# Heads of an mLSTM: weights divided by their denominators before the value products, shared source blocks added and multiplied once

## The chip, the cores and the metric

One core of a Trainium2 chip runs the whole program. The metric is the device time of one execution in microseconds (us). TensorE (PE) multiplies, VectorE (DVE), ScalarE (ACT) and GpSimd (POOL) work element by element, SyncE (SP) and the other queues start DMAs. PEld is the loading of weights into TensorE, which overlaps its matmuls.

## What is computed

The reference is a two-layer network over 256 context and 1024 latent tokens. The part that matters is the second layer's mLSTM: 4 heads of width 512, each scanned forwards and backwards, both directions after the context. In chunks the reference does, per head and direction,

```
s   = (q k^T) * exp(dmat - m_t)            # weights of target t over sources s
num = s @ v  (+ the carried state)
den = sum(s)  (+ the carried state)
h   = num / max(|den|, exp(-m_t))
hm  = h_forward + flip(h_backward)         # prefix_bidir
hn  = (hm - mean(hm)) * rsqrt(var(hm) + eps)   # head_norm, over the head's 512 columns
```

and then `(hn * g + skip * x) * silu(z)` is multiplied by `w_out`.

## The kernel before

The kernel does not carry a state: for each head it forms all weights of a target over all its sources (full quadratic form, with decays). Targets are the 1024 latent tokens in 4 groups q of 256 (`QW`), each of two blocks j of 128. Sources are 10 blocks of 128 tokens, in 5 pairs p: pair 0 is the context, pairs 1 to 4 the latent tokens. A context block is a source in both directions; a latent block before the target's is a source forwards only, one after it backwards only; the target's own block is a source in both, masked. So `sources(q, j, d)` has 13 entries over both directions d, for 10 different blocks.

Every product in fp32 is made of three products of rounded halves (`PARTS`: high*high, high*low, low*high). ACT makes the high part (`high`, L1512) and DVE the low part, full minus high (`low`, L2220). So the weights exist three times in SBUF: `PR` (p_full), `PH` (p_part0), `PL` (p_part1), each with two halves z = q % 2 of 26 pieces of 128 columns.

The head loop (`head` in each engine's program, 4 heads, heads 1 and 2 in a hardware loop) is written out by hand in the same order on every engine:

- `score(i, q, p)`: PE, 24 matmuls of 256 columns: one pair of source blocks against 256 targets, into one of three rotating PSUM banks (`SLOTS`, `LOB`; a slot may be written when what lay three slots before has been read). `value(i, n)` and `queries(i, q)` make values and queries in the same slots, in among the scores of q = 0 and 1 (queries of the next head at the end of the head).
- `weigh(q, p)`: DVE multiplies the scores by the decays into `PR` (L2325 for the target's own pair, L2327 for the others). `sum_up(i, q)`: POOL adds the pieces to `Sp`, one row of sums for each direction (9 instructions for each q, L2619 and L2629).
- `weights_high` (ACT) and `weights_low` (DVE): parts of the weights, each pair one step behind its `weigh`.
- `value_sums(i, q, j)`: PE, 13 entries x 3 parts = 39 matmuls of 512 columns, the two directions into two PSUM banks. `weight_sums`: two fp32 matmuls by a column of ones, the denominators, one column each.
- `head_out(q, j)`: DVE makes the reciprocal of the denominators (L2336 to L2338), ACT scales the forward bank (L1605), DVE adds the scaled backward bank (L2340), `bn_stats` (L2343) and `bn_aggr`, ACT a square root (L1608), DVE normalises (L2354).
- `transposed(i, q, j)` (PE, L1132) and `mixed(i, q, j)` (DVE, L2407, L2410) bring the result out, in among the scores of a later q.
- POOL's `masked` (L2606) and ACT's `decays` (L1587, L1590) prepare the decays of a later q. DVE's `columns_low` and ACT's `columns_high_in` make the parts of the next head's inputs near the end of a head.

The order on PE in one head: scores of q = 0, of q = 1, both value sums of q = 0, then for q = 2 and 3 five scores and both value sums of q - 1, then the queries of the next head around the value sums of q = 3.

## Time and profile before

| what | value |
|---|---|
| time, median of 3 | 2986.97 us (2985.12 to 2987.44) |
| the profiled execution | 2982.24 us |
| its span, first to last instruction | 2980.2 us |
| TensorE busy | 92% of the span |
| VectorE, ScalarE, GpSimd busy | 52%, 28%, 34% |
| mean granted TensorE clock | 0.949 |

The heads lie between about 2118 and 2770 us. In each row of a timeline stand the start in us, the duration, the engine, the line, the operation, output and inputs by name, shape and count; what is in brackets is how long the engine sat idle before it, and what ended that. A run of like instructions stands as one row. An fp32 matmul (not of rounded parts) is recorded as two matmuls.

### The profile page before, as it was taken

Reading aid. Unit: us, or ns where it says so; the run is one execution under the profiler, and the core shown is the slowest. Engines: PE = TensorE matmul, PEld = TensorE weight load, DVE = VectorE, ACT = ScalarE, POOL = GpSimd, SP = SyncE. Lnnn points to the kernel's source line nnn. Section 1 sums busy time; section 2 is a strip of 40 time slices with the busy share of each in tenths; the row PEclk is TensorE's granted clock in tenths of the full one; section 3 lists DMA queues with packets and bytes.
Section 4 is the critical chain, followed back from the end, with each engine's and each line's share of the span. In section 5 each row is a group of like instructions: output and inputs, shape, how many; then the busy total and the mean of one; then the engine's idle time right before and its main releaser. Section 6 shows DMA issues by size and latency. Waiting matters only on the chain.

```text
span 2980.2 us, 38078 instructions
## 1 busy us (share of the span) xinstructions
PE 2748.7 (92%) x13429; PEld 2132.8 (72%) x13429; DVE 1544.2 (52%) x2331; ACT 843.0 (28%) x1004; POOL 1027.7 (34%) x1181
## 2 busy tenths in 40 slices
PE   7998778999898999989995999999899999999998
PEld 5656764444454777878883777777798888888787
DVE  2336875678777121452326444585546555555611
ACT  1213551625625111321213222211323333231310
POOL 0006996878820001021123333343434334333000
PEclk8799889999999998899997999999999999999999
DMA  4512221011013667452103222256313121313521
GB/s 151 178 64 84 85 80 60 21 46 46 28 46 101 198 187 239 117 179 73 32 25 87 99 99 99 92 169 227 138 40 109 65 98 56 114 43 128 167 84 47
DMA packets 258722, 297.92 MB, mean 100 GB/s; under 512 B 34944, under 2 KB 222632, under 8 KB 258224
## 3 DMA queue, kind: packets, MB, share of 16 engines
q1 hardware_dynamic: 203104, 206.75, 21.8%
q10 hardware_dynamic: 50672, 72.89, 6.7%
q0 software_dynamic: 4832, 16.78, 1.9%
q8 instruction: 69, 1.13, 0.2%
q14 instruction: 45, 0.37, 0.0%
HBM read 203.09 MB, written 93.29 MB: 99 GB/s over the span
## 4 chain that ended last, share of the span: by engine, by line
PE 62%; DVE 12%; issue 5%; ACT 3%; POOL 1%; DMA 1%; DVEq 0%; SPq 0%; ACTq 0%; POOLq 0%
PE ps L130 53%; PE ps L1178 5%; PE ps L1027 1%; PE ps L1021 1%; DVE s_scan_tmp L1926 1%; DVE s_scan_tmp L1924 1%; DVE arena L1928 1%; DVE arena L1946 1%; DVE arena L1977 1%; DVE xc_part L2220 1%; DVE arena L1970 1%; DVE arena L485 1%; POOL h_part L2558 0%; PE ps L1183 0%; ACT arena L1342 0%
## 5 line engine op out<-in xcount | busy, mean ns | idle before, releaser
L130 PE MATMUL ps<-arena,weights 128*128 128x512 f32 (+2 forms) x2432 | 753.7, 488 | 51.1 <-ACT arena L1342 19.5
L130 PEld LDWEIGHTS ps<-arena,weights 128*128 128x128 f32 (+1 forms) x2432 | 398.6, 177 | 394.8 <-issue 325.1
L130 PE MATMUL ps<-h_part,in_weight_parts 128*128 128x512 f32 (+1 forms) x1920 | 419.2, 379 | 38.7 <-DVE h_part L1719 14.9
L130 PEld LDWEIGHTS ps<-h_part,in_weight_parts 128*128 128x128 f32 x1920 | 342.0, 192 | 111.3 <-issue 24.3
L130 PE MATMUL ps<-v_part,p_part 128*128 128x512 f32 x1248 | 295.1, 395 | 0.1
L130 PEld LDWEIGHTS ps<-v_part,p_part 128*128 128x128 f32 x1248 | 234.2, 190 | 49.2 <-issue 0.9
L130 PE MATMUL ps<-q_part,xc_part 128*128 128x256 f32 x1920 | 248.1, 288 | 14.7 <-DVE v_part L2220 10.7
L130 PEld LDWEIGHTS ps<-q_part,xc_part 128*128 128x128 f32 x1920 | 237.7, 195 | 16.3 <-DVE v_part L2220 11.5
L1178 PE MATMUL ps<-wo_part,mx_part 128*128 128x512 f32 x768 | 184.0, 400 | 5.2 <-DVE mx_part L2220 4.6
L2547 POOL TENSOR_TENSOR in_weight_parts<-weights,ones 128x1024 fp32r<-128x1024 f32 x32 | 79.2, 2474 | 305.6 <-issue 212.8
L1178 PEld LDWEIGHTS ps<-wo_part,mx_part 128*128 128x128 f32 x768 | 145.4, 191 | 40.0 <-issue 4.8
L2629 POOL TENSOR_TENSOR decays<-decays,p_full 128x256 f32<-128x256 f32 (+1 forms) x128 | 150.6, 1176 | 63.6 <-DVE p_full L2327 36.3
L130 PE MATMUL ps<-ao_part,out_weight_parts 128*128 128x512 f32 (+1 forms) x576 | 116.7, 363 | 8.1 <-DVE ao_part L2004 8.1
L130 PE MATMUL ps<-bo_part,out_weight_parts 128*128 128x512 f32 (+1 forms) x576 | 116.3, 362 | 4.4 <-DVE bo_part L2004 4.4
L2460 POOL TENSOR_TENSOR arena<-arena 128x640 f32 x16 | 31.7, 1979 | 251.0 <-DVE arena L1841 246.1
L2052 DVE SCALAR_TENSOR_TENSOR arena<-ps,modulation,arena 128x256 f32 (+3 forms) x32 | 32.6, 1060 | 159.8 <-PE ps L130 159.8
L130 PEld LDWEIGHTS ps<-ao_part,out_weight_parts 128*128 128x128 f32 x576 | 97.1, 192 | 25.6 <-issue 8.3
L130 PE MATMUL ps<-y_part,out_weight_parts 128*128 128x512 f32 (+1 forms) x576 | 114.9, 362 | 0.0
L1999 DVE COPY arena<-arena 64x1280 f32 x16 | 26.0, 1626 | 168.7 <-PE ps L130 168.4
L130 PE MATMUL ps<-arena 128*128 128x160 f32 (+2 forms) x608 | 108.5, 323 | 4.9 <-ACT arena L1454 2.9
L130 PEld LDWEIGHTS ps<-bo_part,out_weight_parts 128*128 128x128 f32 x576 | 96.4, 190 | 22.2 <-DVE bo_part L2004 2.7
L130 PEld LDWEIGHTS ps<-y_part,out_weight_parts 128*128 128x128 f32 x576 | 96.8, 191 | 17.9
(354 smaller groups left out, 4194.8 us busy)
## 6 DMA issues: line engine op xcount, KB each, us to landing
weights<-in_e_w_in SPq DMA_DIRECT2D x32, 512.0 KB, 4.2
weights<-in_o_w_in SPq DMA_DIRECT2D x32, 512.0 KB, 4.1
s_out_maps<-arena ACTq DMA_DIRECT2D x16, 640.0 KB, 3.0
weights<-in_mod_w POOLq DMA_DIRECT2D x20, 512.0 KB, 4.8
arena<-s_out_maps SPq DMA_DIRECT2D x16, 640.0 KB, 4.3
ml_xcv<-arena ACTq DMA_DIRECT2D x16, 640.0 KB, 3.0
xc_full<-ml_xcv SPq DMA_DIRECT2D x4, 2560.0 KB, 8.9
xm_tiles<-ml_xm SPq DMA_DIRECT2D x16, 640.0 KB, 3.9
```

The lines of the kernel that those rows point to most:

```text
L130: return nc.tensor.matmul(o, lhsT, rhs, start=(k == 0), stop=(k == n - 1))
L485: link(V.scalar_tensor_tensor(out=o, in0=o, scalar=1.0 / (2 * c + 1), in1=z2, op0=ALU.add, op1=ALU.mult))
L1021: nc.tensor.matmul(psG[:, t0:t0 + n], WFs[:, s, 0], xco[:, s, t0:t0 + n], start=False, stop=False, skip_group_check=True)
L1027: last = nc.tensor.matmul(psG[:, t0 + o:t0 + o + r.shape[1]], WFs[:, s, 1], r, start=False, stop=False, skip_group_check=True)
L1178: nc.tensor.matmul(ps[:, 2 * (b % 4) + h], Mbs[x][b % 2][:, k], Wos[w][k][:, BANK * h:BANK * h + BANK], start=(k == 0 and n == 0), stop=Fa ...
L1924: V.tensor_tensor(s2[:, ::-1], z, A2h, ALU.mult).then_inc(sem("scan_v"), 1)
L1926: V.tensor_tensor(s1, s1, s2, ALU.add).then_inc(sem("scan_v"), 1)
L1928: V.tensor_tensor(w, w, s1, ALU.add).then_inc(sem("scan_v"), 1)
L2052: V.scalar_tensor_tensor(out=o, in0=a, scalar=MOD[:, bass.ds(4 * i + (2 * (16 + s) + w), 1)], in1=x, op0=ALU.mult, op1=ALU.add).then_inc(s ...
L2460: GP.tensor_tensor(Gv[s][:, :, 0], pw(0), cc(0), ALU.mult)
L2547: GP.tensor_tensor(WXs[s][:, 0], Wv[:, s], ones[:, :].unsqueeze(1).to_broadcast([P, DT, P]), ALU.mult).then_inc(sem("w_high"), 1)
L2629: GP.tensor_tensor(Sp[:, z, s0:s1], Sp[:, z, s0:s1], PR[:, z, o:o + s1 - s0], ALU.add).then_inc(sem("sums"), 1)
```

## The change

The weights are divided by their denominators before they are multiplied by the values. Then the two directions can be added: for a source block that both directions use, the two weight pieces are added and multiplied by the values once.

- PE: `value_sums` has 10 blocks x 3 parts = 30 matmuls, all into one bank (2 + 2 (q % 2) + j). `weight_sums` becomes `denominators(i, q)`, the same four matmuls by a column, into a slot bank "d", ahead of the value sums. New is `denominator_rows(i, q)`: an fp32 matmul of 512 columns, ones times a 128x512 tile with the reciprocals on diagonals, so that each reciprocal stands in a row over all partitions, in a slot bank "r".
- DVE: `reciprocals(q)` (three small instructions and the diagonals `DG`, 128x512), `rows_out(q)` (PSUM to `RR`, 128x512), `scale_shared(q)` (weights of the pairs 0 and q + 1 times the rows: 1024, 512 and 256 columns), `merge_shared(q)` (additions of 512, 128 and 128 columns, and the other three pairs times their row, 512 each). `weights_low` works on 512 columns for every pair (before 1024, 768 and 3 x 512). In `head_out` the reciprocals and the addition of the directions go; `bn_stats` and the normalisation read PSUM.
- ACT: `weights_high` 5 x 512 columns for each q, from the scaled weights; the scaling in `head_out` goes, the square root stays (`spread`).
- The parts of the weights of q are no longer made one step behind `weigh(q, p)`: those of q = 0 are made after the queries of q = 3, those of q = 1 and 2 in among `weigh(q + 1, p)`, those of q = 3 between the value sums of q = 2.
- 48 slots in a head instead of 40.

```diff
+            def denominator_rows(i, q):
+                pe.wait_ge(*past("den_diag", 4 * i + (q + 1)))
+                mm(slot(i, "r", q), ones[:, :], DG, 0, 1).then_inc(sem("lo_mm"), 1)
+
+            def value_sums(i, q, j, first=0, end=NBLK):
+                if j == 0 and first == 0:
                     pe.wait_ge(*past("pl_ready", 20 * i + (5 * q + 5)))
...
+                for I in range(first, end):
+                    c = QW * (I % 2) + P * j
+                    x = (PH[:, q % 2, QW * (I - I % 2) + c:QW * (I - I % 2) + c + P], PL[:, q % 2, PAIR_AT[q][I // 2][0] + c:PAIR_AT[q][I // 2][0] + c + P])
+                    for m, (a, b) in enumerate(PARTS):
+                        last = mm(ps[:, 2 + 2 * (q % 2) + j], x[a], Vs_[b][:, I], 3 * I + m, 3 * NBLK)
...
                 for p in range(NPR):
                     value(i, p + 6)
                     score(i, 1, p)
+                    if p == 0:
+                        denominators(i, 0)
+                    elif p == 1:
+                        denominator_rows(i, 0)
                 value(i, 11)
                 queries(i, 3)
-                weighted(i, 0)
                 for q in (2, 3):
+                    value_sums(i, q - 2, 0)
+                    denominators(i, q - 1)
+                    value_sums(i, q - 2, 1)
+                    denominator_rows(i, q - 1)
                     for p in range(NPR):
                         score(i, q, p)
                         if p in (2, 4):
                             transposed(i, q - 2, p // 2 - 1)
-                    weighted(i, q - 1)
+                value_sums(i, 2, 0, 0, NBLK // 2)
+                denominators(i, 3)
+                value_sums(i, 2, 0, NBLK // 2, NBLK)
+                denominator_rows(i, 3)
+                value_sums(i, 2, 1)
+                value_sums(i, 3, 0)
                 if not last_head:
                     queries(i + 1, 0)
-                value_sums(i, 3, 0)
                 transposed(i, 2, 0)
...
# ACT, head()
+                for n in range(6, 12):
+                    value_high(i, n)
                 queries_high(i, 3)
+                for n in range(NPR):
+                    weights_high(i, 0, n)
                 decays(i, 3)
...
# DVE
+                def scale_shared(q):
+                    z, a, b = q % 2, PAIR_AT[q][0][0], PAIR_AT[q][q + 1][0]
+                    dve.wait_ge(*past("vq_ev", NEV * i + EVICTED["r", q]))
+                    dve.wait_ge(*past("sums", 36 * i + (9 * q + 9)))
+                    x = PR[:, z, a:a + 4 * QW].rearrange("p (d i t) -> p d i t", d=2, i=2)
+                    V.tensor_tensor(x, x, rd.unsqueeze(2).to_broadcast([P, 2, 2, QW]), ALU.mult)
+                    V.tensor_tensor(PR[:, z, b:b + 2 * QW], PR[:, z, b:b + 2 * QW], RR, ALU.mult)
+                    ilink(V.tensor_tensor(PR[:, z, b + 2 * QW:b + 3 * QW], PR[:, z, b + 2 * QW:b + 3 * QW], RR[:, P:P + QW], ALU.mult))
...
                 for p in range(NPR):
+                    if p == 2:
+                        rows_out(0)
                     value_low(p + 6)
                     weigh(1, p)
+                    if p == 0:
+                        reciprocals(0)
+                    elif p == 2:
+                        scale_shared(0)
+                    elif p == 3:
+                        merge_shared(0)
                 value_low(11)
...
-                weights_low(1, NPR - 1)
-                for q in (0, 1):
-                    head_out(q, 0)
-                    head_out(q, 1)
+                for n in range(NPR):
+                    weights_low(0, n)
+                for q in (1, 2):
+                    head_out(q - 1, 0)
+                    reciprocals(q)
+                    head_out(q - 1, 1)
+                    rows_out(q)
                     for p in range(NPR):
-                        weigh(q + 2, p)
+                        weigh(q + 1, p)
+                        if p == 0:
+                            scale_shared(q)
+                        elif p == 1:
+                            merge_shared(q)
                         if p in (2, 4):
-                            mixed(i, q, p // 2 - 1)
-                    weights_low(q + 2, NPR - 1)
+                            mixed(i, q - 1, p // 2 - 1)
+                        if p in (2, 3):
+                            weights_low(q, 2 * p - 4)
+                            weights_low(q, 2 * p - 3)
+                    weights_low(q, 4)
+                reciprocals(3)
                 head_out(2, 0)
+                rows_out(3)
+                scale_shared(3)
+                merge_shared(3)
+                for n in range(NPR):
+                    weights_low(3, n)
+                head_out(2, 1)
                 if not last_head:
                     maps_low(i + 1)
                     columns_low(i + 1)
-                head_out(2, 1)
```

## Rows read from the trace of the kernel before

**Rows 1.** Busy time by stretch: length, engines with counts, clock, DMA share, GB/s.

```profile
2450.00:2610.00 160.00, 152.06 (x978) 138.16 (x978) 90.14 (x189) 50.84 (x86) 60.09 (x56) 0.99 0.24 81
```

**Rows 2.** Waits in the heads, PE: us in total, times, longest.

```profile
PE ps L130 <- DVE v_part L2220: 14.4, 7, 3.3
```

**Rows 3.** Groups: count | busy us, mean ns of one | idle before them.

```profile
L130 PE MATMUL ps<-v_part,p_part 128*128 128x512 f32 x1248 | 295.1, 395 | 0.1
```

**Rows 4.** Timeline, head 1, PE: value sums of q 0, scores of q 2.

```profile
2338.04 9.13 PE L130 MATMUL ps<-v_part,p_part 128*128 128x512 f32 x39
...
2347.01 0.50 PE L130 MATMUL ps<-ones,decays 128*128 128x1 f32 x4
...
2347.37 9.15 PE L130 MATMUL ps<-v_part,p_part 128*128 128x512 f32 x39
...
2356.72 8.88 PE L130 MATMUL ps<-q_part,xc_part 128*128 128x256 f32 x72
...
2371.97 9.12 PE L130 MATMUL ps<-v_part,p_part 128*128 128x512 f32 x39
```

**Rows 5.** Timeline, earlier stage: fp32 matmuls of 512 columns, each recorded twice.

```profile
1881.90 1.02 PE L1021 MATMUL ps<-arena 128*128 128x512 f32 x2
1882.76 1.02 PE L1027 MATMUL ps<-arena 128*128 128x512 f32 x2
```

**Rows 6.** Timeline, head 1, DVE: from the statistics of q 0 onwards.

```profile
2359.06 0.69 DVE L2343 BATCH_NORM_STATS2 att_small<-weights 128x6 f32<-128x512 f32 x1
...
2360.60 1.00 DVE L2354 TENSOR_SCALAR weights<-weights,s_scan_tmp 128x512 f32<-128x512 f32 x2
2361.52 2.43 DVE L2327 SCALAR_TENSOR_TENSOR p_full<-ps,att_small,decays 128x256 f32<-128x256 f32 x6
...
2367.33 0.69 DVE L2220 TENSOR_TENSOR p_part<-p_full,p_part 128x512 fp32r<-128x512 f32 x1 [0.66 <-POOL decays L2629]
2367.94 0.68 DVE L2407 TENSOR_TENSOR weights<-ps,weights 128x512 f32<-128x512 f32 x1
```

**Rows 7.** Groups of VectorE, by shape.

```profile
L2220 DVE TENSOR_TENSOR p_part<-p_full,p_part 128x512 fp32r<-128x512 f32 x48 | 34.9, 726 | 8.5 <-POOL decays L2629 5.5 <-ACT p_part L1512 2.9
...
L2220 DVE TENSOR_TENSOR p_part<-p_full,p_part 128x1024 fp32r<-128x1024 f32 x16 | 19.5, 1220 | 5.6 <-POOL decays L2619 5.6
...
L2354 DVE TENSOR_SCALAR weights<-weights,s_scan_tmp 128x512 f32<-128x512 f32 x32 | 16.0, 543 | 0.6
...
L1701 DVE COPY arena<-ps 128x512 f32<-128x512 f32 x16 | 10.5, 687 | 23.6 <-PE ps L770 23.6
```

**Rows 8.** Timeline, head 3, PE: queries of q 2 to the first value sum.

```profile
2632.11 1.66 PE L130 MATMUL ps<-xc_part,qk_map_part 128*128 128x256 f32 x12
...
2636.04 3.10 PE L130 MATMUL ps<-q_part,xc_part 128*128 128x256 f32 x24 [1.37 <-DVE q_part L2260]
...
2642.48 3.13 PE L130 MATMUL ps<-q_part,xc_part 128*128 128x256 f32 x24 [2.45 <-DVE v_part L2220]
...
2658.42 9.10 PE L130 MATMUL ps<-v_part,p_part 128*128 128x512 f32 x39
```

**Rows 9.** Timeline, head 1, PE: value sums of q 2 to the next head.

```profile
2405.89 9.12 PE L130 MATMUL ps<-v_part,p_part 128*128 128x512 f32 x39
...
2440.20 0.60 PE L130 MATMUL ps<-ones,decays 128*128 128x1 f32 x4 [1.57 <-DVE weights L2407]
...
2451.77 2.05 PE L130 MATMUL ps<-s_decay,xm_tiles 128*128 128x128 f32 x16 [1.63 <-issue]
```

**Rows 10.** Timeline, head 1, PE: a score behind a wait.

```profile
2320.55 4.65 PE L130 MATMUL ps<-q_part,xc_part 128*128 128x256 f32 x24 [2.52 <-DVE v_part L2220]
```

**Rows 11.** Busy time by stretch, same place; clock is third from the right.

```profile
2320.50:2323.50 3.00, 2.95 (x14) 2.95 (x15) 2.16 (x5) 1.06 (x1) 1.28 (x1) 0.52 0.13 42
```

**Rows 12.** Timeline, head 1: POOL's additions, an addition of DVE beside others.

```profile
2403.89 1.85 POOL L2629 TENSOR_TENSOR decays<-decays,p_full 128x256 f32<-128x256 f32 x2 [0.54 <-DVE p_full L2327]
...
2408.12 1.60 DVE L2410 TENSOR_TENSOR weights<-weights 128x1024 f32<-128x1024 f32 x1
```

More of the change, by code:

```diff
@@ L350, in build @@
         EVICTED = {x: sum(y[0] != "s" for y in SLOTS[:n + 1]) for n, x in enumerate(SLOTS)}
+        HIGHS = {x: sum(y[0] in "qv" for y in SLOTS[:n + 1]) for n, x in enumerate(SLOTS)}
+        NEV = EVICTED["r", 3]
         LOB = (0, 1, 7)
-        assert LO == 40 and [x for x in SLOTS if x[0] == "s"] == [("s", q, p) for q in range(NQ) for p in range(NPR)]
+        assert LO == 48 and NEV == 28 and [x for x in SLOTS if x[0] == "s"] == [("s", q, p) for q in range(NQ) for p in range(NPR)]
         def slot_bank(*x):
@@ L402, in pair_pieces @@
             if p == 0:
-                return [(I, d, 0, QW) for I in range(2) for d in range(2)]
+                return [(I, d, 0, QW) for d in range(2) for I in range(2)]
             if 2 * p == J0:
@@ L1111, in weight_sums @@
-            def weight_sums(i, q, j):
-                u0 = isinstance(i, int) and i == 0 and q == 0
-                if j == 1:
-                    pe.wait_ge(*past("rd_ready", 8 * i + (2 * q + 1)))
-                elif not u0:
-                    pe.wait_ge(*past("mx_ev", 8 * i + 2 * q))
-                for d in range(2):
-                    c = QW * d + P * j
-                    last = mm(ps[:, 6, 2 * j + d:2 * j + d + 1], Sp[:, q % 2, c:c + P], ones[:, 0:1], 0, 1)
-                last.then_inc(sem("pv_mm"), 1)
@@ L1122, in weighted, with denominators @@
-            def weighted(i, q):
-                for j in range(2):
-                    value_sums(i, q, j)
-                    weight_sums(i, q, j)
+            def denominators(i, q):
+                pe.wait_ge(*past("sums", 36 * i + (9 * q + 9)))
+                o = slot(i, "d", q)
+                for j in range(2):
+                    for d in range(2):
+                        c = QW * d + P * j
+                        last = mm(o[:, 2 * j + d:2 * j + d + 1], Sp[:, q % 2, c:c + P], ones[:, 0:1], 0, 1)
+                last.then_inc(sem("lo_mm"), 1)
@@ L1649, in head @@
                     columns_high_in(i + 1)
-                head_out(i, 2, 1)
-                if not last:
                     first_queries(i + 1)
@@ L1655, in head @@
                         out_weights_high(k)
-                head_out(i, 3, 0)
-                if last:
                     for b in range(2):
                         block_high(b)
-                head_out(i, 3, 1)
+                spread(i, 3)
             first_queries(0)
@@ L2215, in _ @@
                 link(last)
-            n0, per = link_n[0], 16
+            n0, per = link_n[0], 12
             def low(o, x, h, name):
@@ L2307, in weigh, with weights_low @@
+                def weights_low(q, n):
+                    p = ORDER[q][n]
+                    a = PAIR_AT[q][p][0]
+                    dve.wait_ge(*past("ph_ready", 20 * i + (5 * q + n + 1)))
+                    low(PL[:, q % 2, a:a + 2 * QW], PR[:, q % 2, a:a + 2 * QW], PH[:, q % 2, 2 * QW * p:2 * QW * p + 2 * QW], "pl_ready")
                 def weigh(q, p):
```

152 lines of the change are left out of this document (71 added, 81 removed).

## The prediction

> **What bounds the kernel now.** I read the page first: TensorE is busy for 92% of the span (the table of before). The change touches only the heads, so I then read a stretch of 160 us there, one head long: PE is busy for 152 us of it, DVE for 90, POOL for 60 [rows 1]. The list of waits shows that PE waits little in the four heads: 14.4 us on the low parts of the values is the largest entry [rows 2]. So the heads are bound by PE. The timeline shows that DVE's rest lies in large pieces, while the value sums run. That shape matters: DVE is free during the value sums, but its work between the end of one pair of value sums and the start of the next is a chain, and the change lengthens exactly that chain. So I don't use shares; I lay the new order out by hand against the rows, one stretch of a head after another, in distances from start to start, and sum it against the profiled execution, 2982.24 us.
>
> **PE's work.** A value sum and its two column matmuls take 9.33 us (2338.04 to 2347.37), of which the 39 matmuls take 8.97 (to 2347.01), so 0.230 us each (1248 of them in the group [rows 3], the times from [rows 4]). 30 instead of 39 take 6.90: 2.07 less, 32 times, is 66.2 us, 16.6 in a head. The column matmuls (0.36 us for two) are the same number in other places. New is the fp32 matmul of 512 columns, 0.86 us from one start to the next [rows 5], 4 in a head: 3.4. Net 13.1 us less in a head, 52.5 in all, if nothing waits.
>
> **Stretch C and D, from the value sums of q = 0 (1) to those of q = 1 (2).** Before: 2338.04 to 2371.97, 33.93 us, without a wait; five scores and two transposes in it are 15.25 (2356.72 to 2371.97) [rows 4]. New on PE: 2 x 6.90 + 0.72 + 0.86 + 15.25 = 30.6. New on DVE, counted from the end of the second value sum: 0.2 until it sees it; statistics to normalisation 1.54 (2359.06 to 2360.60) [rows 6]; two normalisations that now read PSUM, 1.3 instead of 0.92 (I take the 0.687 of the copy from PSUM, not the 0.543 of the row from SBUF [rows 7]); `rows_out` 0.6 (the same copy, overlapped); `weigh` of the first pair 1.6 and of each later pair 0.8, the target's own 1.06 (six instructions 2.43 [rows 6]); `scale_shared` 1.15 + 0.61 + 0.42 + a bubble 0.05 = 2.2; `merge_shared` 4 x 0.61 + 2 x 0.2 = 2.85; five `weights_low` at 0.61 (2367.33 to 2367.94 [rows 6]) = 3.1; two transposed tiles out 0.7 each and the addition of 1024 columns 1.15 (1.22 alone [rows 7], less the overlap). In the order of the diff: 0.2 + 1.54 + 1.3 + 0.6 + 1.6 + 2.2 + 0.8 + 2.85 + 0.8 + 0.65 + 1.2 + 1.1 + 1.2 + 0.85 + 1.85 + 0.7 = 19.45 us, and only then has PE the last low part that `value_sums` waits for. PE's own work after the second value sum is 0.86 + 15.25 = 16.1. So PE waits 3.35 us, and the stretch is 6.90 + 0.72 + 6.90 + 19.45 = 34.0 us: nothing gained. DVE's free time lies before, under the value sums, where the new work can't go, because it needs the reciprocals of a slot and stands behind `head_out(q - 1, 1)` on DVE's queue.
>
> **Stretch B, from the queries of q = 2 to the first value sum.** Before 26.3 us (2632.11 to 2658.42), with waits of 1.37 and 2.45 in it [rows 8]. New: `reciprocals(0)` and `merge_shared(0)` stand on DVE ahead of `value_low`, which frees slots. By hand: waits around the first two scores 0.7 + 3.3 + 0.85 and 0.1 before the queries, together 1.2 more than before; column matmuls 0.72 that come here from elsewhere; the row matmul 0.86. The largest is the end: ACT makes all five high parts of q = 0 only after the queries of q = 3. PE ends at 29.85; the last query's high part 0.65 later, five high parts of 512 columns in 2.95, the last low part 0.7: PE waits 4.35. Before, this was hidden in the scores. Sum: 7.15 more.
>
> **Stretch E, from the value sums of q = 2 to the next head.** Before 45.9 (2405.89 to 2451.77) with waits of 1.57 before columns and 1.63 at the loop's edge [rows 9]. New: 8.3 less for four value sums, 0.7 less for columns that moved to B, 0.86 more for rows, and the wait before the columns shrinks by 1.2, since no bank is shared with the transposes there. Against it, from the end of the first value sum of q = 2: `head_out` 1.2, `rows_out` 0.6, 2.2 + 2.85, five low parts 3.1, so 10.0 against 0.86 + 6.90 on PE: a wait of 2.25. Sum: 7.1 less. **Stretch A**, scores of q = 0: `head_out` of q = 3 is about 1.5 us shorter, which removes a wait of 0.7.
>
> Sum in a head at full clock: -0.7 + 7.15 + 0.05 + 0.05 - 7.1 = -0.5 us. The 13.1 are eaten by 12.6 us of new waits.
>
> **The clock.** Behind a wait of 2.52 us a score took 4.65 us [rows 10], where others take 3.10 to 3.13 [rows 8]: 1.5 us lost; the granted clock there was 0.52 [rows 11], that is 1.2 instead of 2.4 GHz. In the heads of before, PE's timeline has five waits of 2.3 to 3.3 us; three had this behind them, two (one is the 2.45 of [rows 8]) had not. Each head now has waits of 4.35, 3.35 and 3.35 us in front of value sums. I take 1.6 us for each of the three: 4.8 in a head. Bounds: 0 if the clock stays, 6.4 if the waits of 3.3 in B and 2.25 in E bring it more often too. By the Trainium skill, "TensorE: Matmul & The Clock Gate", section "Why this matters for your kernels", idle gaps of PE between bursts of matmuls are to be avoided because they bring the clock back to half; the trace agrees, and it speaks against this change, which turns steady work into bursts. Without it the forecast would be the balance below.
>
> **POOL beside DVE.** Two additions of 256 columns on POOL took 1.85 us with DVE quiet there; an addition of 1024 columns on DVE that met others of them took 1.60 [rows 12] instead of 1.22 [rows 7]. The new multiplications and additions have both inputs in SBUF and fall into the time in which POOL sums the next q. From none to about 5.5 us in a head (0.4 for each of some 14 that meet an addition); the 512-column row shows 0.726 on the mean [rows 7] against 0.69 in a quiet place [rows 6], so the low end is nearer: I take 2. The Trainium skill, "SBUF — State Buffer", section "Who interferes with whom", says that a DVE instruction with two inputs in SBUF and a GpSimd instruction that reads SBUF shut each other out for the whole instruction; the trace agrees in kind. By the strict rule the sum would be at the upper end.
>
> **Sum.** -0.5 + 4.8 + 2 = 6.3 us in a head, 25.2 in four; 1.3 more, an estimate, because the first head has no wait in A to lose and the last has no loop's edge and no queries behind it, so 26.5. 2982.2 + 26.5 = 3008.7 for the profiled execution; the median of the runs lies 4.7 above it, so 3013.5.
>
> **Rivals.** (1) *Balance.* The clock stays up and POOL costs nothing: -0.5 in a head, 2985 to 2988, no change. For it: two of the five waits passed without a fall. Against: those were the 2.45 [rows 8] and one like it, and the new ones are longer. It also holds if only one of the two costs comes: up to about 3000. (2) *DVE's chain hides, faster.* The one place is C and D: the 19.45 us chain against 16.1 of PE. If the chain is 16.1 or shorter, both waits go with their clock loss, 6.7 us in a head at full clock; with the wait in E gone as well the heads take 7 to 9 us less each, 2950 to 2960. The point is 3.35 us of chain, a sixth of it; the durations behind it are rows of the same shapes, which vary by 5%, so I give it little. (3) *The removed matmuls count in full*, waits hidden: 2987 - 52 = 2935. It needs also the wait of 4.35 to be wrong, where ACT's order alone makes it. (4) *Ports heavy*: 5.5 instead of 2 for POOL and 6.4 for the clock: 11.4 in a head, 3034.
>
> **How the numbers follow.** Forecast 3005 to 3025: 0.50. (4) and beyond, 3025 and more: 0.14. (1) with one cost only, 2993 to 3005: 0.11; full balance, 2981 to 2993: 0.13. (2) 0.09, (3) 0.03. A measurement of this kernel tells about 0.2% (6 us) from no change. Faster 0.12, same 0.13, slower 0.75. The range must leave out no more than 0.2: from 2970, between balance and (2), to 3040, just beyond (4).
>
> **What would show it.** In the profile after: 960 matmuls of values instead of 1248, at 0.230 each; a row of waits of PE on the low parts of the weights (L2220 of p_part), near 4.4 before the first and 3.3 before the second and third pair of value sums of each head, four times; the granted clock at about 0.5 behind them; DVE without a break from the end of a second value sum to the next first one, 19 to 22 us. Wrong would be: those waits absent or under 1.5 us (the chain is mis-sized), or present at full clock (the clock step fails), or a head that lasts 160 us and less.

## The result, and the profile after

| kernel | median us (lowest to highest) | ratio to before, 95% interval |
|---|---|---|
| before | 2986.64 (2985.12 to 2987.44) | 1 |
| changed | 3066.86 (3066.14 to 3068.85) | 1.027 (1.0252 to 1.0288) |
| predicted | 3013.5 (2970 to 3040) | 1.009 |

The change costs 80 us. The sign was forecast, the size was three times the forecast and lies outside the range. The first group of the page is the value sums, the counterpart of [rows 3]; the waits of TensorE in the four heads follow, the counterpart of [rows 2] (us in all, times, longest).

```profile
L130 PE MATMUL ps<-v_part,p_part 128*128 128x512 f32 x960 | 257.4, 430 | 94.1 <-DVE p_part L2215 94.1
...
PE ps L130 <- DVE p_part L2215: 94.1, 16, 8.0
PE ps L130 <- DVE v_part L2215: 24.6, 14, 3.5
```

The matmuls have gone as planned: 960 for 1248. Their busy time is only 37.7 us less, since the mean of one rose from 395 to 430 ns (the clock, below). And the idle time in front of them went from 0.1 to 94.1 us, in 16 waits, four in each head, all on the low parts of the weights. Head 1 on TensorE, the counterpart of [rows 4], [rows 8] and [rows 9]:

```profile
2327.84 1.67 PE L130 MATMUL ps<-xc_part,qk_map_part 128*128 128x256 f32 x12
...
2338.66 2.08 PE L130 MATMUL ps<-s_decay,xm_tiles 128*128 128x128 f32 x8 [3.54 <-DVE v_part L2215]
...
2354.94 3.13 PE L130 MATMUL ps<-q_part,xc_part 128*128 128x256 f32 x24 [1.09 <-DVE v_part L2215]
...
2360.22 1.76 PE L130 MATMUL ps<-xc_part,qk_map_part 128*128 128x256 f32 x12 [1.71 <-DVE v_part L2215]
2367.62 8.71 PE L130 MATMUL ps<-v_part,p_part 128*128 128x512 f32 x30 [5.64 <-DVE p_part L2215]
...
2408.22 8.90 PE L130 MATMUL ps<-v_part,p_part 128*128 128x512 f32 x30 [8.01 <-DVE p_part L2215]
...
2417.77 7.11 PE L130 MATMUL ps<-v_part,p_part 128*128 128x512 f32 x30
...
2449.00 5.58 PE L130 MATMUL ps<-v_part,p_part 128*128 128x512 f32 x15 [8.01 <-DVE p_part L2215]
...
2468.81 8.76 PE L130 MATMUL ps<-v_part,p_part 128*128 128x512 f32 x30 [2.17 <-DVE p_part L2215]
```

The last row has a wait of 2.17 us; the waits of 8.01 are where the prediction had 3.35. The row of 15 matmuls is half a value sum. A value sum behind a wait takes 8.7 to 8.9 us, the next one 7.11. The clock of these moments (third number from the right), first behind two waits, then in the value sum that follows:

```profile
2367.60:2370.90 3.30, 3.28 (x8) 2.64 (x9) 0.00 (x0) 2.25 (x4) 0.00 (x0) 0.50 0.00 0
2408.20:2411.50 3.30, 3.29 (x8) 2.64 (x9) 0.00 (x0) 0.00 (x0) 0.00 (x0) 0.50 0.44 151
2417.80:2421.00 3.20, 3.20 (x15) 2.64 (x16) 1.38 (x7) 0.00 (x0) 0.00 (x0) 1.00 0.00 0
```

8 matmuls in 3.3 us at 0.50 (1.2 GHz), 15 in 3.2 us at 1.00 (2.4 GHz): the loss is 1.6 to 1.9 us behind each of these waits, near the 1.6 of the forecast. In the last head it is larger, 2.3 to 2.8 us.

Stretch by stretch, head 1, start to start in us (the column of the forecast is the prediction's sum with its 1.6 us of clock, without its 2 us for POOL):

| stretch | before | forecast | after |
|---|---|---|---|
| A, scores of q = 0 | 20.8 | 20.1 | 20.6 |
| B, to the first value sum | 27.9 | 33.5 | 39.8 |
| C, value sums of q = 0, scores of q = 2 | 33.9 | 35.6 | 40.6 |
| D, the same one q later | 33.9 | 35.6 | 40.8 |
| E, to the next head | 45.9 | 40.4 | 40.2 |
| head | 162.4 | 165.2 | 182.0 |

The forecast of B starts from the 26.3 us of head 3, as the prediction does; head 1 had 27.9 before, with 1.5 us of clock loss in it. C, D and B are 5.0, 5.2 and 6.3 us too long; E is 0.2 us off. What VectorE and GpSimd do in D shows why. Below is VectorE from the normalisation of q = 1 to the last low part, with some of GpSimd's additions beside it:

```profile
2426.45 1.53 DVE L2378 TENSOR_SCALAR weights<-ps,s_scan_tmp 128x512 f32<-128x512 f32 x2
...
2430.47 2.12 POOL L2667 TENSOR_TENSOR decays<-p_full 128x512 f32<-128x512 f32 x1 [22.86 <-DVE p_full L2359]
2431.36 1.78 DVE L2320 TENSOR_TENSOR p_full<-p_full,den_rows 128x512 f32<-128x512 f32 x1
...
2434.63 1.99 POOL L2677 TENSOR_TENSOR decays<-decays,p_full 128x256 f32<-128x256 f32 x2 [2.04 <-DVE p_full L2359]
2434.99 0.83 DVE L2326 TENSOR_TENSOR p_full<-p_full 128x128 f32<-128x128 f32 x1
2435.74 0.28 DVE L2327 TENSOR_TENSOR p_full<-p_full 128x128 f32<-128x128 f32 x1
...
2439.32 1.87 POOL L2677 TENSOR_TENSOR decays<-decays,p_full 128x256 f32<-128x256 f32 x2 [2.70 <-DVE p_full L2359]
2439.68 2.05 DVE L2215 TENSOR_TENSOR p_part<-p_full,p_part 128x512 fp32r<-128x512 f32 x2
...
2445.47 2.93 POOL L2677 TENSOR_TENSOR decays<-decays,p_full 128x512 f32<-128x512 f32 x2 [0.64 <-DVE p_full L2357]
2445.95 1.87 DVE L2457 TENSOR_TENSOR weights<-weights 128x1024 f32<-128x1024 f32 x1
2447.74 1.21 DVE L2215 TENSOR_TENSOR p_part<-p_full,p_part 128x512 fp32r<-128x512 f32 x1
```

Two twins stand side by side: the additions of 128 columns, L2326 and L2327, take 0.83 and 0.28 us. The first begins 0.36 us after an addition of GpSimd (2434.63) and lasts until that one is over. The second lies beside GpSimd's next addition and isn't delayed: here an overlap cost VectorE only where it came second. A piece of 512 columns takes 1.78 (L2320) where 0.61 to 0.69 is its own. From the first statistics (2424.91) to the end of the last low part (2448.95) the chain is 24.0 us instead of the 19.45 of the prediction, which has another 0.2 us ahead of the statistics in it.

### The profile page after: what moved, and what is told of

It reads as the page before. It is cut to its first block, busy times and chain, and to the rows that moved or that the text cites. A ratio compares the mean times of both kernels' runs of the same rounds, so it can differ in the third digit from the quotient of the medians.

```text
span 3064.8 us, 37650 instructions
## 1 busy us (share of the span) xinstructions
PE 2728.6 (89%) x13173; PEld 2108.0 (69%) x13173; DVE 1653.4 (54%) x2427; ACT 811.9 (26%) x972; POOL 999.9 (33%) x1181
## 4 chain that ended last, share of the span: by engine, by line
PE 57%; DVE 16%; issue 6%; ACT 4%; DMA 1%; POOL 1%; DVEq 0%; SPq 0%; ACTq 0%; POOLq 0%
PE ps L130 49%; PE ps L1185 5%; DVE p_part L2215 2%; PE ps L1028 1%; PE ps L1022 1%; DVE p_full L2359 1%; DVE p_full L2331 1%; DVE arena L1923 1%; DVE s_scan_tmp L1919 1%; DVE s_scan_tmp L1921 1%; DVE arena L486 1%; ACT decays L1598 1%; DVE p_full L2320 1%; DVE weights L2454 1%; DVE p_full L2319 0%
## 5 line engine op out<-in xcount | busy, mean ns | idle before, releaser
L130 PE MATMUL ps<-v_part,p_part 128*128 128x512 f32 x960 | 257.4, 430 | 94.1 <-DVE p_part L2215 94.1
L130 PEld LDWEIGHTS ps<-v_part,p_part 128*128 128x128 f32 x960 | 198.3, 210 | 143.7 <-DVE p_part L2215 86.8
L2677 POOL TENSOR_TENSOR decays<-decays,p_full 128x256 f32<-128x256 f32 (+1 forms) x128 | 130.4, 1019 | 138.7 <-DVE p_full L2359 103.6
```

The lines of the kernel that those rows point to most:

```text
L130: return nc.tensor.matmul(o, lhsT, rhs, start=(k == 0), stop=(k == n - 1))
L2677: GP.tensor_tensor(Sp[:, z, s0:s1], Sp[:, z, s0:s1], PR[:, z, o:o + s1 - s0], ALU.add).then_inc(sem("sums"), 1)
```

## The experiments

The first theory was that sentence: VectorE's chain of C and D is stretched by GpSimd, and PE waits for it in full. The rivals: the chain is too long even alone; the place of the low parts and not the new multiplications makes the wait; ScalarE's order makes the wait in B; the clock makes it all worse.

### GpSimd's sums cut to one column

```diff
-GP.tensor_tensor(Sp[:, z, s0:s1], Sp[:, z, s0:s1], PR[:, z, o:o + s1 - s0], ALU.add)
+GP.tensor_tensor(Sp[:, z, s0:s0 + 1], Sp[:, z, s0:s0 + 1], PR[:, z, o:o + 1], ALU.add)
```

> The changed kernel, with POOL's additions of the weights of the pairs 1 to 4 cut to one column each (so the denominators hold the context's weights alone; everything else is done as before on whole tiles). Ports theory: TensorE's waits of 8.0 us before the second and third pair of value sums are my hand-laid chain of 19.5 us plus some 4.5 us in which DVE and POOL shut each other out of SBUF. Then those waits fall to 3.0 to 4.5 us, the first low parts of a pair take 0.61 us from start to start instead of 1.0, the 512-column scaling 0.68 instead of 1.5, and the kernel takes 30 to 50 us less than the changed one (3067), so 3017 to 3037. Rival, the new instructions are slow by their shapes and operands: the waits stay at 7 to 8 us, the time within 8 us of 3067.

Measured: 3022.25 us, ratio 1.012 (1.01 to 1.0141), 45 us less than the changed kernel. The waits in front of the value sums of head 1 are 4.85, 4.44, 4.63 and 2.44 us (5.64, 8.01, 8.01, 2.17 before the edit). VectorE in D:

```profile
2406.60 0.70 DVE L2365 BATCH_NORM_STATS2 att_small<-ps 128x6 f32<-128x512 f32 x1 [5.60 <-PE ps L130]
...
2413.04 1.78 DVE L2320 TENSOR_TENSOR p_full<-p_full,den_rows 128x512 f32<-128x512 f32 x1
...
2416.67 0.28 DVE L2326 TENSOR_TENSOR p_full<-p_full 128x128 f32<-128x128 f32 x1
...
2426.37 0.89 DVE L2215 TENSOR_TENSOR p_part<-p_full,p_part 128x512 fp32r<-128x512 f32 x1
```

The chain is 20.7 us (2406.60 to 2427.26). L2326 is down to 0.28. One piece still takes 1.78: it meets the first pair's addition, which this edit left whole. Without that 1.1 us the chain is 19.6, near the 19.45 that was added up. So the chain alone was sized rightly, and GpSimd's price in D is 3.4 + 1.1 = 4.5 us; the wait shows the same 3.4 (8.01 to 4.63).

45 of the 80 us go with GpSimd's additions of the weights. By stretches, start to start in head 1, they are 4.3 us in B (39.8 to 35.5), 3.6 in C, 3.5 in D, none in A and -0.4 in E. In C and D the time is in VectorE's instructions, as shown. In B a part of it is another thing: ScalarE's decays wait for GpSimd itself, 3.68 us in the changed kernel, and the value parts behind them wait too. The two were not separated there.

### TensorE kept busy during the waits

```diff
+for n in range((16, 28, 28, 0)[q]):
+    mm(ps[:, 3 + 2 * (q % 2)], Vs_[0][:, 0, 0:P], Vs_[0][:, 1], 0, 1)
 pe.wait_ge(*past("pl_ready", 20 * i + (5 * q + 5)))
```

> The changed kernel with extra matmuls (512 columns, values by values, into a bank that is overwritten afterwards) in front of TensorE's wait for the last low part: 16 before the value sums of q = 0, 28 before those of q = 1 and 2, 3.7 and 6.4 us of work that fits into the waits of 5.5 and 8 us. Clock theory: each of these waits is followed by some 3 us at half the clock, 1.6 us lost; with the extra work the first 30 matmuls of a pair take 7.0 to 7.1 us instead of 8.4 to 8.9, and the kernel 12 x 1.5 = 15 to 20 us less, 3047 to 3052. Rival, the value sums behind a wait are slow for another reason (operands fetched anew, the port): no gain, 3067 or a little more.

Measured: 3043.07 us, ratio 1.019 (1.017 to 1.0211), 24 us less, more than the 15 to 20 that were expected. Behind what is left of the waits (1.84, 1.70 and 1.68 us) the value sums run at full clock, here the first of them:

```profile
2361.70:2365.00 3.30, 3.25 (x14) 2.67 (x15) 0.00 (x0) 2.45 (x5) 0.00 (x0) 1.00 0.03 5
```

They take 7.11 to 7.14 us. The twelve sums behind these waits took 22.8 us more than at full clock in the changed kernel. The fourth wait of a head, some 2.1 us, was left as it was, and the clock fell behind it in three heads of the changed kernel and in none here (7.07 to 7.14 for 8.71 to 8.76): another 4.9 us. A few other places got slower, such as a sum of 8.69 behind 1.88 us of waiting. The clock is a cost of its own, and it isn't the main one.

### The rows between the two value sums

The row matmul goes ahead of the second value sum of a q, so that scaling and merging run under it (C and D only). Scaling and merging leave their places behind `weigh`, and ScalarE's square roots go behind its high parts:

```diff
-                    value_sums(i, q - 2, 0)
+                    value_sums(i, q - 2, 0, 0, NBLK // 2)
                     denominators(i, q - 1)
-                    value_sums(i, q - 2, 1)
+                    value_sums(i, q - 2, 0, NBLK // 2, NBLK)
                     denominator_rows(i, q - 1)
+                    value_sums(i, q - 2, 1)
...
-                    head_out(q - 1, 0)
                     reciprocals(q)
-                    head_out(q - 1, 1)
+                    head_out(q - 1, 0)
                     rows_out(q)
+                    scale_shared(q)
+                    merge_shared(q)
+                    head_out(q - 1, 1)
```

> The changed kernel with the row matmul of q = 1 and 2 between the two value sums instead of behind the second (denominators after the first half of the first), so that DVE copies, scales and merges while the second value sum runs, when POOL has nothing to do; only the statistics, the weighing, the low parts and the mixing stay in the chain. Chain theory: 24.1 us of chain lose 5.7 us of work and most of the 4.5 us of mutual exclusion, 14 to 16 us are left against 16 us of TensorE's work, so the waits of 8 us and the clock loss behind them go: 8 x (8 + 1.6) = 77 us less, 2985 to 3000. If the work is merely moved (DVE's sum decides, not its place), less than 20 us go.

Measured: 3039.42 us, ratio 1.0185 (1.0168 to 1.0202). 27 us less, where 67 to 82 were expected: the waits of C and D fell from 8.01 to 4.18 and 4.44 us and not to nothing. The scaling and merging now run with GpSimd idle, at their own speed (1.22, 0.69, 0.42, 0.69, 0.28, 0.28, and 1.89 for three). What is left is the tail:

```profile
2386.70 1.88 POOL L2676 TENSOR_TENSOR decays<-decays,p_full 128x256 f32<-128x256 f32 x2 [1.33 <-DVE p_full L2360]
2387.05 2.08 DVE L2216 TENSOR_TENSOR p_part<-p_full,p_part 128x512 fp32r<-128x512 f32 x2
...
2390.12 2.38 DVE L2216 TENSOR_TENSOR p_part<-p_full,p_part 128x512 fp32r<-128x512 f32 x2
...
2395.17 1.21 DVE L2216 TENSOR_TENSOR p_part<-p_full,p_part 128x512 fp32r<-128x512 f32 x1
2396.43 5.30 PE L130 MATMUL ps<-v_part,p_part 128*128 128x512 f32 x15 [4.18 <-DVE p_part L2216]
```

The low parts stand behind the third, fourth and fifth `weigh`, which themselves wait for TensorE's scores. However early the scaling is, they can't be earlier. And GpSimd is in this tail as well: the five low parts take 5.67 us here and 3.46 in the first experiment, so of the 4.18 us of wait some 2.2 are collisions again.

### No scaling and merging at all

To see that tail without the rest: the multiplications and additions of the weights cut to one column each, everything else as in the changed kernel (the weights stay undivided).

```diff
-V.tensor_tensor(x, x, rd.unsqueeze(2).to_broadcast([P, 2, 2, QW]), ALU.mult)
...
+V.tensor_tensor(PR[:, z, c:c + 1], PR[:, z, c:c + 1], RR[:, 0:1], ALU.mult).then_inc(sem("scaled"), 1)
```

> The changed kernel with the multiplications and additions of the weights by the rows cut to one column each (the weights are then neither divided nor merged; all else is done). It prices DVE's new work on the path: the chain of 24 us loses 5 us of work and 2 to 4 us of mutual exclusion and ends within 1 us of TensorE's 16, so the waits of 8 us fall to 1 to 2.5 us without a clock loss, the wait of 2.2 us near the end of a head goes, and the one of 5.6 us falls to 4.3, which is ScalarE's order alone. 2960 to 2985. Rival, the waits have another cause (the low parts' place alone): they stay above 4 us, 3015 and more.

Measured: 3013.96 us, ratio 1.010 (1.008 to 1.0121); the theory's 2960 to 2985 was missed, the rival held.

```profile
2390.96 8.70 PE L130 MATMUL ps<-v_part,p_part 128*128 128x512 f32 x30 [4.18 <-DVE p_part L2216]
...
2427.97 5.81 PE L130 MATMUL ps<-v_part,p_part 128*128 128x512 f32 x15 [4.44 <-DVE p_part L2216]
```

4.18 and 4.44 us: to the hundredth the waits of the run before. With most of the 5.1 us of scaling and merging taken from the chain the wait shrinks by 3.8 and then stands still. So there are two limits, one behind the other: the chain from the second value sum (8.01), and the place of the low parts with the collisions they meet there (4.2 to 4.4). No run has the rows early and GpSimd's sums cut; by the durations above the place alone would leave some 2 us, an estimate. The prediction's rival 2, "if the chain is 16.1 or shorter, both waits go", was wrong as a statement about this order.

### The low parts two pairs earlier

On top of the rows' new place, the low parts of q = 1 and 2 come behind the `weigh` of pairs 0, 1 and 2:

```diff
+                        if p in (0, 1):
+                            weights_low(q, 2 * p)
+                            weights_low(q, 2 * p + 1)
+                        elif p == 2:
+                            weights_low(q, 4)
...
-                        if p in (2, 3):
-                            weights_low(q, 2 * p - 4)
-                            weights_low(q, 2 * p - 3)
-                    weights_low(q, 4)
```

> The kernel with the rows early (3039) and, besides, the low parts of the weights of q = 1 and 2 made behind the weighing of the first, second and third pair instead of the third, fourth and fifth, where DVE had idle stretches of 1 and 2 us. Chain theory: the waits of 4.2 and 4.4 us before the second and third pair of value sums were made by where the low parts stand, since DVE is idle earlier in the same stretch; they go, and the 1.6 us of clock behind each: 8 x 5.9 = 47 us less, 2988 to 2998. If DVE's and POOL's amount of work decides there, at least half of the waits stays: 3015 and more.

Measured: 3005.31 us, ratio 1.0074 (1.0057 to 1.0091). 34 us less than with the rows moved alone, 62 less than the changed kernel.

```profile
2350.95 5.05 PE L130 MATMUL ps<-v_part,p_part 128*128 128x512 f32 x15 [5.64 <-DVE p_part L2216]
...
2383.07 3.67 PE L130 MATMUL ps<-v_part,p_part 128*128 128x512 f32 x15
...
2413.81 3.67 PE L130 MATMUL ps<-v_part,p_part 128*128 128x512 f32 x15
...
2435.63 8.76 PE L130 MATMUL ps<-v_part,p_part 128*128 128x512 f32 x30 [5.27 <-DVE p_part L2216]
```

D is 30.7 us (2383.07 to 2413.81), with no wait at either end: exactly the 30.6 that the prediction has for TensorE alone. Collisions are still there (two low parts take 2.13 us), only nobody waits for them. It missed the expected 2988 to 2998, and the wait in E grew from 2.61 in the run before to 5.27. The trace shows what came into that chain: GpSimd's eight masked additions for the next head (2426.28, 6.93 us) now lie beside the merging and the low parts. In the changed kernel they were over (2457.87) before that chain began (2458.97).

### ScalarE's order in B

```diff
+                value_high(i, 6)
+                value_high(i, 7)
                 decays(i, 2)
-                for n in range(6, 12):
+                for n in range(8, 11):
                     value_high(i, n)
-                queries_high(i, 3)
                 for n in range(NPR):
                     weights_high(i, 0, n)
+                value_high(i, 11)
+                queries_high(i, 3)
```

(VectorE's low parts in the same order.)

> The changed kernel with another order on ScalarE and VectorE between the queries of q = 2 and the first value sum: two value parts ahead of the decays that wait for POOL, and the high and low parts of the weights of q = 0 ahead of the last queries instead of behind them. Order theory: the wait of 3.5 us before the value matmuls and most of the 5.6 us before the first value sum are made by this order alone, with 1.6 us of clock behind each: 5 to 9 us less in each head, 3030 to 3047. Rival, DVE's amount of work in this stretch decides: the wait only moves, 3060 to 3067.

Measured: 3046.37 us, ratio 1.0206 (1.0189 to 1.0223), 20 us less. The wait of 3.54 in B is gone, 5.64 is 4.13. So 5 us in each head are the order of the parts on ScalarE and VectorE; the waits of 1.10, 1.70 and 4.13 stay. The part of this edit that the kernel before can take, decays behind two value parts instead of ahead:

```diff
-                decays(i, 2)
                 value_high(i, 6)
                 for p in range(NPR):
                     value_high(i, p + 7)
+                    if p == 0:
+                        decays(i, 2)
                     weights_high(i, 1, p)
```

> The kernel before, with two value parts on ScalarE ahead of the decays that wait for POOL: the part of the reordering that has nothing to do with the change. The wait of 2.5 to 3.3 us before the second score of q = 1 goes, and the clock loss behind it in two of four heads: 10 to 13 us less, 2972 to 2978. If another wait takes its place, no change. What the reordered kernels gain over this one is what the change itself gives.

Measured: 2969.03 us, ratio 0.9953 (0.9936 to 0.9969). That is 16 us less than the kernel before in the same set of runs (2985.07), and 3 less than the lower end of what was expected. So some 16 us of what the next kernels gain have nothing to do with the change, and the fair kernel to hold them against is this one.

### All chains moved

Rows early in B too, scaling and merging one pair earlier there, the parts of q = 0 among the last pairs, both orders from above.

> The same and, in the stretch of q = 1, denominators ahead of the first score, the row matmul ahead of the second, scaling and merging one pair earlier, the high and low parts of q = 0 in among the last pairs, and two value parts on ScalarE ahead of the decays. Order theory: the waits of 3.5, 1.1, 1.7 and 5.6 us in this stretch and the clock behind two of them shrink to 1 to 3 us in sum, 9 to 13 us less in each head: 2940 to 2960, faster than the kernel before. This would show the change to be worth 1% with another order. If the work itself is too much, the wait before the first value sum stays at 3 us or more: 2970 and more.

Measured: 2951.10 us, ratio 0.9894 (0.9877 to 0.991): 1.1% faster than before, and 0.6% faster than the kernel before with ScalarE's order mended. The waits on the low parts of the weights are 25.9 us in 8: 2.06 in front of the first value sum and 5.39 in E.

### Stretch E, and GpSimd out of its way

In E, first only the order of TensorE and VectorE:

```diff
-                value_sums(i, 2, 0, NBLK // 2, NBLK)
+                value_sums(i, 2, 0, NBLK // 2, NBLK - 2)
                 denominator_rows(i, 3)
+                value_sums(i, 2, 0, NBLK - 2, NBLK)
...
                 reciprocals(3)
-                head_out(2, 0)
                 rows_out(3)
...
+                head_out(2, 0)
                 head_out(2, 1)
```

> Everything of the run with all chains moved (2951.1 us), and stretch E as well: the row matmul of q = 3 two source blocks before the end of the first value sum, and on VectorE nothing of the statistics of q = 2 ahead of the copy, the scaling, the merging and the low parts of q = 3. There TensorE waited 5.39 us on the last low part before the first value sum of q = 3. The copy of the rows can start some 1.9 us earlier. Theory (the wait in E is VectorE's chain behind the row matmul, nothing else): the wait falls to about 3.5 us in each head, 1.9 x 4 = 7.6 us less, 2942 to 2946 us. Rival (something else sets the end there, or the statistics moved behind it come too late for what follows): the time stays within 2 us of 2951.

Measured: 2946.05 us, ratio 0.9874 (0.9858 to 0.9891); the wait is 3.75. That is the upper edge of the theory's band (2942 to 2946). Then, on top of it, GpSimd's masked additions for the next head wait until the low parts of q = 3 are made:

```diff
                 for k in range(2):
                     value_weight(i, k)
+                if not (isinstance(i, int) and i == 0):
+                    pool.wait_ge(*past("pl_ready", 20 * i))
                 for q in range(2):
                     masked(i, q)
```

> The same, and GpSimd begins the eight masked additions for the next head (6.98 us, in the middle of the chain of stretch E) only when the last low part of q = 3 is made. They are the only work of GpSimd that VectorE's chain meets there. Theory (an instruction of VectorE with two inputs in SBUF waits for the whole GpSimd addition it meets): the additions of 128 columns fall from 0.83 to near 0.3 us, the three multiplications from 0.99 to 0.65, the five low parts from 0.83 to 0.65: 1.1 + 1.0 + 0.9 = 3.0 us of chain, the wait before the first value sum of q = 3 is about 0.5 us and its clock loss of 1.7 goes with it: 3.0 to 4.7 us in each of three heads, 9 to 14 us less than the previous kernel, 2929 to 2936 us. Rival (contention is weak, the pieces are long for another reason): 2 us less or none.

Measured: 2936.86 us, ratio 0.9839 (0.9822 to 0.9855), 9.2 us less: at the lower end of the theory's difference, 0.9 above its band. The additions of 128 columns, which were to fall from 0.83 us, took 0.28 in both. Against the kernel before with ScalarE's order mended it is 32 us, 1.1%. The order of every instruction on VectorE is the same with the masked additions early and late. First the kernel with the masked additions early, then with them late:

```profile
2402.66 2.98 DVE L2339 TENSOR_TENSOR p_full<-p_full,den_rows 128x512 f32<-128x512 f32 x3
2402.70 8.11 POOL L2661 TENSOR_TENSOR decays<-xb_rows,att_small 128x256 f32<-128x256 f32 x8 [7.58 <-DMA xb_rows<-ml_rows]
2405.56 4.94 DVE L2223 TENSOR_TENSOR p_part<-p_full,p_part 128x512 fp32r<-128x512 f32 x5
...
2410.56 8.58 PE L130 MATMUL ps<-v_part,p_part 128*128 128x512 f32 x30 [3.75 <-DVE p_part L2223]
```

```profile
2397.87 1.89 DVE L2339 TENSOR_TENSOR p_full<-p_full,den_rows 128x512 f32<-128x512 f32 x3
2399.68 3.09 DVE L2223 TENSOR_TENSOR p_part<-p_full,p_part 128x512 fp32r<-128x512 f32 x5
...
2402.82 7.11 PE L130 MATMUL ps<-v_part,p_part 128*128 128x512 f32 x30 [0.83 <-DVE p_part L2223]
2403.02 6.20 POOL L2661 TENSOR_TENSOR decays<-xb_rows,att_small 128x256 f32<-128x256 f32 x8 [12.72 <-DVE p_part L2223]
```

Eight pieces take 4.98 us instead of 7.92, the wait falls from 3.75 to 0.83, the same 2.9, and the clock loss goes with it (8.58 to 7.11). GpSimd is faster too, 6.20 for 8.11, though other work of VectorE lies beside it there: each engine was slower where they met. This is the cleanest pair of the study. In it nothing is left out, and one engine's start is all that differs.

### What GpSimd still costs then

The last kernel with GpSimd's sums cut to one column, as in the first experiment.

> The same, and GpSimd's additions of the pieces of pairs 1 to 4 cut to one column (the sums of the weights are left out but for their first pair and one column). What is left of the price of GpSimd beside VectorE is then seen: with all chains moved, TensorE waits about 2.1 us before the first value sum of a head and nothing elsewhere on low parts. Theory (the moved order hides nearly all that GpSimd costs, and the rest is the one wait before the first value sum with the clock behind it): 2 to 3.8 us in each head, 8 to 15 us less than the previous kernel, 2917 to 2927 us. Rival (collisions still cost where no wait is seen, in many short delays): 25 us less or more, under 2910. Second rival (nothing left): within 4 us of the previous kernel.

Measured: 2936.04 us, ratio 0.9835 (0.9819 to 0.9852): 0.8 us less, no difference. The theory's 2 to 3.8 us in each head was wrong, the second rival held. The collisions are there, as the low parts of the weights show, first with the whole sums, then with one column:

```profile
L2223 DVE TENSOR_TENSOR p_part<-p_full,p_part 128x512 fp32r<-128x512 f32 x80 | 64.1, 840 | 0.0
```

```profile
L2223 DVE TENSOR_TENSOR p_part<-p_full,p_part 128x512 fp32r<-128x512 f32 x80 | 55.1, 729 | 0.0
```

These parts are 9.0 us shorter in the four heads, and the time is the same. It is a balance: TensorE's waits on low parts of the weights fell from 11.0 to 9.4 us and its waits on the sums themselves (2.2 us) went, while its waits on value parts rose from 6.1 to 7.7 us, with one of 3.80 us where 2.58 had been. The same edit was worth 45 us in the changed kernel. The price of a collision is decided by what waits behind it.

## Why the prediction was wrong, point by point

- *TensorE's work, 52.5 us less.* Right. 960 matmuls; with no wait, D is 30.7 us against 30.6 worked out.
- *The chain of 19.45 us in C and D.* Right as a sum of VectorE alone: 19.6 by the first experiment. Its waits would have been 3.35 us; 4.63 with one collision of 1.1 left in.
- *POOL beside VectorE, 2 us in a head.* This step failed. GpSimd's additions cost 11 us in a head (10.9 in head 1: 4.3 in B, 3.6 in C, 3.5 in D, -0.4 in E), and that with one addition in each q left whole. Part of the 4.3 in B is ScalarE's wait for GpSimd and no collision. The prediction had both ends before it, 0 and 5.5, and took the lower since a group of many low parts had a mean of 0.726 against 0.69 [rows 7]. But those pieces were kept out of GpSimd's way: in the kernel before `weights_low` waits for the semaphore of GpSimd's sums (`sums`) before it starts, and [rows 7] shows idle time ended by them. The changed kernel has no such wait in `weights_low`; the mean there is 0.939. The price of a piece that does meet an addition stood in the same trace, 1.60 for 1.22 [rows 12], and even it was too small for a bound: the rest of a whole addition is waited for, 0.4 to 1.1 us for each. The 1.85 us beside it was not read in a quiet place either, since a low part of VectorE (2403.65, 0.68 us) lies in it; in quieter places of the changed kernel two such additions took 1.54 to 1.56. The Trainium skill, "SBUF — State Buffer", section "Who interferes with whom", has this as an exclusive lock; the durations here agree, and the strict rule that was weighed and put aside was the one that held. The upper end of 5.5 was too low as well, since each collision was priced at 0.4.
- *Order on VectorE as one sum.* The text took it that only the total of the chain counts. There is a second limit behind it, the low parts behind the third to fifth `weigh` (4.2 to 4.4 us of wait with the scaling and merging cut). It didn't change the time here, but it made rival 2 wrong, and the expectation of the rows' experiment with it.
- *Stretch B, +7.15 us.* Half right. The waits 0.80 and 3.54 are the 0.7 and 3.3 by hand. 1.09 and 1.71 later were 0.95 in all, the last was 5.64 and not 4.35, and behind 3.54 the clock fell: from 2338.66 to 2344.85 TensorE did in 6.19 us what it does in 3.77 elsewhere. 3.5 + 2.4 of the 6.3 us are these; the prediction knew the wait and gave it no clock, except in a bound. Of the 1.3 that the last wait was too long, 1.05 are GpSimd again: the five low parts took 4.14 us beside its masked additions, 3.09 in stretch E.

```profile
2362.61 3.64 POOL L2653 TENSOR_TENSOR decays<-xb_rows,att_small 128x256 f32<-128x256 f32 x4
2363.25 4.14 DVE L2215 TENSOR_TENSOR p_part<-p_full,p_part 128x512 fp32r<-128x512 f32 x5
```

- *The clock, 1.6 us behind each of three waits.* Right in size behind each (1.6 to 1.9), too small in sum: it fell behind 3.54 and behind 2.17 as well, so that head 1 lost 9.3 us by it and not 4.8. The prediction had looked only at waits of 2.3 us and more in the kernel before; there too the clock fell behind a shorter one, 1.57 us (last section).
- *Stretch E, 7.1 less; A, 0.7 less.* E is right to 0.2 us, in part by luck. Its wait is 2.17 for 2.25, with GpSimd idle in that chain. But the 1.65 us of clock behind that wait were not forecast, and about as much went that was not forecast either: a wait of 0.98 on the next head's inputs, and 0.96 of the 1.63 at the loop's edge. A is 0.2 less.
- *Sum.* Head 1 took 19.6 us more than before, where the forecast had 6.3. The four heads took 181.1, 182.0, 183.5 and 182.0 us for 162.7, 162.4, 159.5 and 159.2: 84.8 us together, counted to the first matmul behind the heads, which is all of the difference between the two profiled executions (84.6). Of the 13.3 that head 1 was off, 8.9 are GpSimd's term and 4.5 the clock's. The two are read from different rows and overlap with the smaller errors, so they are sizes and not a closed sum. The larger one lies on a place where the prediction itself had shown that every microsecond counts in full.

The rivals: 4, ports heavy with more clock, was the right mechanism, at 11.4 us in a head instead of 19.6. It was given 0.14 with everything above it.

With both orders and the rows moved, B's last wait is 2.06 us. 0.4 of it are GpSimd's sums (1.66 in the last kernel); what makes the rest was not tried.

## What to carry to other kernels

Before work is moved from TensorE to VectorE, add up the chain between the last value it needs and the first matmul that needs it, and then look at what GpSimd does in exactly that time: each instruction of VectorE with both inputs in SBUF that meets one of GpSimd is to be priced at what may be left of that whole instruction, not by the mean of its group. A group's mean says nothing if the order before kept the two apart; look for the wait that did it. A collision, like a wait, is worth nothing or everything by its place: the same sums on GpSimd cost 45 us in one order and nothing that could be measured in another. And a change that saves work can be right and still lose with its first order: here the same arithmetic is 2.7% slower or 1.6% faster than before (0.5% of the latter by ScalarE's order alone).

## What the runs showed of the hardware

- VectorE and GpSimd: an addition of 128 columns on VectorE took 0.28 us alone and 0.83 when it began inside one of GpSimd; 512 columns 0.61 to 0.69 and up to 1.78. GpSimd's eight masked additions took 4.48 to 9.96 us in different kernels; in the one pair that differs in nothing else, 8.11 and 6.20. VectorE's `weigh`, which has one input in PSUM, kept its time beside GpSimd's additions (0.86 to 0.88 for two of 256 columns). This is what the Trainium skill, "SBUF — State Buffer", section "Who interferes with whom", says of VectorE's instructions with two inputs in SBUF and of those with one.
- Normalising 512 columns out of PSUM takes 805 ns on the mean in the changed kernel, from SBUF 543 [rows 7]; as a pair 1.53 us against 1.00 [rows 6]. The forecast had 1.3.

```profile
L2378 DVE TENSOR_SCALAR weights<-ps,s_scan_tmp 128x512 f32<-128x512 f32 x32 | 24.5, 805 | 0.8
```

- The granted clock fell behind all waits of 3.5 us and more on low parts that were read. Between 1.57 and 3.50 us both happened, even in one and the same kernel: in the changed one a value sum behind 2.08 us took 8.71 in the first head and 7.10 in the last; in the one with the masked additions late, the half sum behind 2.06 took 3.71 in head 1 and 5.30 in head 2. It fell even behind 1.85 us (a score of 4.64 for 3.12, changed kernel, head 2) and, in the kernel before, behind 1.57 us: below are value sums in heads 1 and 2, granted clock 1.00 and 0.52. So the length of a wait alone didn't decide it.

```profile
2440.67 9.13 PE L130 MATMUL ps<-v_part,p_part 128*128 128x512 f32 x39
...
2600.36 10.72 PE L130 MATMUL ps<-v_part,p_part 128*128 128x512 f32 x39
```
